# Hand-over rewrite of the stages behind the attention, and another order of the prologue, in a two-block transformer kernel

## The chip, the cores and the metric

The kernel runs on one core of a Trainium2 chip. The metric is the device time of one execution in microseconds (us), as the median of several runs. TensorE is called PE here, VectorE DVE, ScalarE ACT, GpSimd POOL, and SyncE, which issues most of the transfers, SP.

## The reference, cut to what matters

512 tokens of 1024 features pass through two blocks. In the first, 16 learned tokens are put in front, so 528 positions are projected.

```python
def first_block(...):                       # one layer
    u = rmsnorm(h, pre_norm_g)
    proj = u @ w_in                         # 1024 -> cq, ckv, k_pe, z_mla, fq, fk, fv, f_logit, z_fox, gate_a, gate_b
    q = rmsnorm(cq) @ w_uq; kv = rmsnorm(ckv) @ w_ukv        # 16 heads, rotary part of 32
    o_mla = causal_attention(q, k, v)
    cum = cumsum(log_sigmoid(f_logit + fox_forget_b))         # forget gate, enters the second attention
    o_fox = causal_attention(fq, fk, fv, cum)
    mixed = (sigmoid(gate_a) * ((o_mla * silu(z_mla)) @ w_br_mla)
             + sigmoid(gate_b) * ((o_fox * silu(z_fox)) @ w_br_fox)) @ w_out
    return (h + rmsnorm(mixed, post_norm_g))[:, 16:]

def second_block(x, ...):                   # two layers
    # layer 0: xn @ w_in_even -> gated 3-tap convolution (a) and multiscale pooling (b); @ w_out_even; + h
    # then the feed-forward: silu(conv3(hn @ w_gate) + b) * (hn @ w_up), @ w_down; + h   (width 2816)
    # layer 1: gelu(xn @ w_in_odd) -> u, v; gate = tril(w_spatial) @ rms_norm(v) + b_spatial; (u * gate) @ w_out_odd; + h
    # then a feed-forward again
    return rms_norm(h, final_norm)
```

Everything is float32. A product is made exact enough by splitting both operands into a rounded part (HI) and a rest (LO), and adding three products: HI·HI, HI·LO and LO·HI.

## The kernel before, in words

Activations lie transposed: features on the 128 partitions, tokens along the free dimension, as 8 tiles `[128, 512]` (`KT = 8`). A weight **unit** is a panel of 128 output columns by 1024 inputs. `w_load` (SP, L254) brings a unit into one of two raw buffers once the unit two before it has been split, `w_hi` (ACT, L291) rounds it to HI, `w_lo` (DVE, or POOL during the attention, L302) makes LO, and `product` (PE, L331) runs 8 k-tiles by 3 passes, 24 matmuls of 512 columns. Each engine has one program in order; all order between engines is in semaphores, written out by hand. `loop` runs the first and the last body straight and the rest in a hardware loop. The stages in order are:

- **Prologue** (`load_prologue`, `act_prologue`, `pool_prologue`, `dve_prologue`, `pe_prologue`). ACT issues the constants, the meta tokens and the 13 small tables (gains, convolution taps: `dma_small`, L367 to L381), SP issues x and the weights. PE waits for all small tables (L608), transposes them, then the meta tokens (L615), then x (L623, 32 transposes); DVE scales the rows of x (`normalise`, L507), ACT and DVE make HI and LO of the normalised x (`u`). Four units follow: two for cq, one for the forget gate with the rotary key, one for ckv. The forget gate is finished only in `dve_first` and `act_first` of step 0.
- **Steps** 0 to 16 (`steps`): in each, PE interleaves the scores and values of one pair of heads with the projections of the next. Step 0 has no attention and fills q, k, v of pair 0; its DVE program starts with the rotary key's LO (`dve_kpe_lo`, L584), its POOL program makes LO of the rotated queries (L1270) before it splits the first unit of step 1. Step 16 has the last pair and the two gate products of the first mix tile.
- **Mix** (`pe_mix`, `act_mix`, `dve_mix`): 16 gated attention tiles are split (L1423, L1457), then 4 units per output tile.
- **Out** (`pe_out`, `act_out`, `dve_out`): 8 units; x is read again (`x2_in`, behind `mixed`) and transposed (L1654); the squares of the result are added up by POOL (`pool_squares`, L1595), summed over partitions on PE (L1660), turned into 1/rms per token, put on a diagonal and broadcast by PE into bank 7 (L1663). Then DVE runs, for each of 8 tiles, scale (L1714), add (L1716), and LO (`h_low`, L1707).
- **Even** (`pe_even`, `act_even`, `dve_even`): 4 units for the pooling branch, 3, then the pool unit, then 9 for the convolution branch. The broadcast 1/rms comes from a matmul of ones with `acc` (`pe_stats`), a square root and a DVE reciprocal of 512 columns (L1622).
- **Residual products** (`pe_residual` and its companions), **feed-forward** (`*_ffn`), **odd** (`*_odd`: v, spatial weights, u, then the gate: DVE L2147, DVE L2154 multiply by u, ACT L2106 HI, DVE L2161 LO; 2 buffers `odt`), and **final** (`pe_final`, `act_final`, `dve_final`, `load_final`: 32 transposes L2187, ACT scales by 1/rms L2202, DVE multiplies by the gain L2212, SP writes 4 tiles of 512 KB, L2175).

The lines of `out` that the text comes back to:

```python
for n in range(KT):                                   # dve_out
    ...
    dve.tensor_tensor(res_t[:, n % 2, :], m2[:, n, :], bank(7), ALU.mult).then_inc(sem("res"), 1)
    dve.wait_ge(sem("res"), n + 1)
    dve.scalar_tensor_tensor(out=h[:, n, :], in0=res_t[:, n % 2, :], scalar=vcol("post_g", n),
                             in1=h[:, n, :], op0=ALU.mult, op1=ALU.add).then_inc(sem("h_tile"), 1)
    if n:
        h_low(n - 1)
```

## Time and profile before

| | |
|---|---|
| median of 3 runs | 1854.63 us (1853.55 to 1855.92) |
| profiled execution, its own time | 1852.69 us |
| its span, first to last instruction | 1851.0 us |
| PE busy | 1781.2 us, 96% of the span |
| DVE, ACT, POOL busy | 926.5, 766.2, 353.4 us |
| mean granted TensorE clock | 0.987 of full speed |
| DMA | 150.65 MB, 81 GB/s over the span |

The profile is one execution as the hardware profiler saw it. A row of the timeline gives the start, the duration, engine, line, operation, count, and in square brackets how long the engine had been idle before it and who ended that. PE is busy nearly always, so what matters are the stretches in which it is idle, or in which its granted clock is at half: those are read by stage.

### The profile page before, as it was taken

The page shows a single profiled execution, that of the slowest core. Times are in us where ns is not written, and L with a number is a line of the kernel's source. Part 1 is how long each engine was busy: PE and PEld are TensorE (multiplying, and loading weights), DVE is VectorE, ACT ScalarE, POOL GpSimd, SP SyncE. Part 2 cuts the span into 40 slices and gives each one's busy share as a digit, 9 for nine tenths or more (in the row PEclk, how much of TensorE's full clock was granted, in tenths as well). Part 3 has the DMA queues.
Part 4 walks back from the last instruction along what each step waited for, and adds up shares of the span by engine and source line. Part 5 has one row for each costly group of instructions (what it writes and reads, how often), then busy time and mean ns, then how long its engine had stood idle before and what let it go on. Part 6 is the DMA issues. An engine that isn't in the chain of part 4 may idle for free.

```text
span 1851.0 us, 25382 instructions
## 1 busy us (share of the span) xinstructions
PE 1781.2 (96%) x8785; PEld 1475.3 (80%) x8785; DVE 926.5 (50%) x1465; ACT 766.2 (41%) x1332; POOL 353.4 (19%) x383
## 2 busy tenths in 40 slices
PE   7899999999999999979999999999999999999998
PEld 6677778898987888757778888888787878888886
DVE  4656565555555334386555555433336455555322
ACT  4656565554544223333343333322263443333222
POOL 4534435333321000220021111101000211111000
PEclk9999999999999999989999999999999999999998
DMA  4111112121212333413333333333331333333332
GB/s 128 51 42 38 52 42 58 47 59 46 57 46 69 102 91 86 142 46 97 91 91 91 96 96 91 99 95 93 110 93 57 91 98 95 91 101 91 94 95 96
DMA packets 282071, 150.65 MB, mean 81 GB/s; under 512 B 11735, under 2 KB 277970, under 8 KB 282002
## 3 DMA queue, kind: packets, MB, share of 16 engines
q1 hardware_dynamic: 280912, 149.14, 27.9%
q8 instruction: 42, 0.69, 0.2%
q10 hardware_dynamic: 546, 0.40, 0.1%
q0 software_dynamic: 544, 0.20, 0.1%
q14 instruction: 27, 0.22, 0.0%
HBM read 147.54 MB, written 2.16 MB: 81 GB/s over the span
## 4 chain that ended last, share of the span: by engine, by line
PE 85%; DVE 8%; ACT 3%; issue 2%; DMA 1%; POOL 1%; ACTq 0%; POOLq 0%; DVEq 0%; SPq 0%
PE ps L331 65%; PE ps L889 5%; PE ps L770 3%; PE ps L2029 2%; PE ps L747 2%; PE ps L729 2%; PE ps L736 1%; ACT w_split L291 1%; DVE w_split L302 1%; PE ps L776 1%; DVE arena_r L1170 1%; PE ps L783 1%; DVE tmp L1622 1%; DVE u L1707 0%; DVE arena_r L1140 0%
## 5 line engine op out<-in xcount | busy, mean ns | idle before, releaser
L331 PE MATMUL ps<-u,w_split 128*128 128x512 f32 x3888 | 925.2, 396 | 17.2 <-DVE u L1707 7.9
L331 PEld LDWEIGHTS ps<-u,w_split 128*128 128x128 f32 x3888 | 726.2, 189 | 185.3 <-issue 11.3
L302 DVE TENSOR_TENSOR w_split<-w_raw,w_split 128x1024 fp32r<-128x1024 f32 (+1 forms) x221 | 266.8, 1208 | 475.8 <-ACT w_split L291 475.8
L291 ACT CAST w_split<-w_raw 128x1024 fp32r<-128x1024 f32 (+4 forms) x321 | 288.5, 913 | 420.6 <-PE ps L331 353.6
L331 PE MATMUL ps<-arena_r,w_split 128*128 128x512 f32 x1824 | 420.9, 392 | 7.2 <-DVE arena_r L2161 3.0
L331 PEld LDWEIGHTS ps<-arena_r,w_split 128*128 128x128 f32 x1824 | 344.6, 189 | 81.6 <-DVE arena_r L2161 4.8
L302 POOL TENSOR_TENSOR w_split<-w_raw,w_split 128x1024 fp32r<-128x1024 f32 (+3 forms) x100 | 138.1, 1401 | 47.0 <-ACT w_split L291 46.8
L1951 POOL TENSOR_TENSOR tmp<-tmp 128x512 f32<-128x512 f32 x44 | 56.9, 1294 | 424.8 <-ACT tmp L1936 424.8
L955 ACT ACTIVATE tmp<-ps,stats 128x144 f32<-128x144 f32 (+3 forms) x128 | 69.3, 541 | 145.8 <-DVE stats L1127 145.3
L1595 POOL TENSOR_TENSOR tmp<-tmp 128x512 f32<-128x512 f32 x42 | 63.3, 1506 | 281.4 <-ACT tmp L1558 246.5
L889 PE MATMUL ps<-u,w_split 128*128 128x264 f32 x768 | 104.4, 288 | 0.5 <-POOL w_split L302 0.5
L1140 DVE TENSOR_TENSOR arena_r<-ps,arena_r 128x128 fp32r<-128x128 f32 (+3 forms) x128 | 62.8, 491 | 73.2 <-ACT arena_r L971 72.3
L889 PEld LDWEIGHTS ps<-u,w_split 128*128 128x128 f32 x768 | 97.0, 189 | 1.5 <-POOL w_split L302 0.9
L1127 DVE TENSOR_REDUCE stats<-ps 128x1 f32<-128x144 f32 (+3 forms) x128 | 64.3, 502 | 51.3 <-PE ps L731 50.5
L1592 POOL COPY tmp<-tmp 128x512 f32<-128x512 f32 x6 | 4.9, 823 | 439.1 <-ACT tmp L1558 253.3
L1308 POOL TENSOR_TENSOR tmp<-tmp,ones 128x16 f32<-128x16 f32 x128 | 28.2, 220 | 279.7 <-DVE tmp L1135 278.7
L971 ACT CAST arena_r<-ps 128x128 fp32r<-128x128 f32 (+3 forms) x128 | 54.4, 425 | 56.8 <-PE ps L747 55.4
L770 PE MATMUL ps<-arena_r 128*128 128x512 f32 (+3 forms) x384 | 71.9, 329 | 2.4 <-DVE arena_r L1140 2.4
L1936 ACT ACTIVATE tmp<-tmp,vec 128x512 f32<-128x512 f32 x44 | 31.8, 723 | 97.7 <-DVE tmp L1972 97.7
L1972 DVE SCALAR_TENSOR_TENSOR tmp<-tmp,vec 128x512 f32<-128x512 f32 x88 | 65.9, 749 | 5.5 <-DVE tmp L1972 0.3
L770 PEld LDWEIGHTS ps<-arena_r 128*128 128x128 f32 x384 | 58.8, 189 | 8.9 <-DVE arena_r L1140 4.3
L1942 ACT CAST arena_r<-tmp 128x512 f32 (+1 forms) x44 | 27.3, 620 | 87.2 <-DVE tmp L1982 87.2
(233 smaller groups left out, 1541.4 us busy)
## 6 DMA issues: line engine op xcount, KB each, us to landing
w_raw<-in_w_in_dram SPq DMA_DIRECT2D x118, 256.0 KB, 3.1
w_raw<-in_w_ffn_gate_dram SPq DMA_DIRECT2D x88, 256.0 KB, 3.1
w_raw<-in_w_ffn_up_dram SPq DMA_DIRECT2D x88, 256.0 KB, 3.2
w_raw<-in_w_ffn_down_dram SPq DMA_DIRECT2D x64, 256.0 KB, 3.1
w_raw<-in_w_in_even_dram SPq DMA_DIRECT2D x32, 256.0 KB, 3.0
w_raw<-in_w_in_odd_dram SPq DMA_DIRECT2D x32, 256.0 KB, 3.1
w_raw<-in_w_ffn_down_dram SPq DMA_DIRECT2D x32, 192.0 KB, 2.7
w_raw<-in_w_br_mla_dram SPq DMA_DIRECT2D x16, 256.0 KB, 3.1
```

The costliest lines, as they stand in the source:

```text
L291: ins = act.copy(dst, src)
L302: ins = dve.tensor_tensor(lo, r, hi, ALU.subtract)
L331: last = pe.matmul(out_ap, w_tile(c, ws, k - n0), moving(k, ms), start=start and n == 0, stop=stop and n == len(total) - 1, skip_group_che ...
L770: pe.matmul(bank(B_O, j * P, 512), v_t[:, par, vs, j, v_cols(hh)], p_t[:, hh, pp * NQ + j, j * P:512], start=hh == 0 and j == 0 and n == 0 ...
L889: ins = pe.matmul(bank(b, 0, HALF), w_tile(c + j, ws, k), u[:, k, ms, half * HALF:(half + 1) * HALF], start=k == 0 and n == 0, stop=k == K ...
L955: act.activation(probs(b), scored(b), ACT.Exp, bias=neg[:, b:b + 1], accum_out=rs[:, b:b + 1]) \
L971: act.copy(hi, src).then_inc(sem("p_hi"), 1)
L1127: dve.tensor_reduce(neg[:, b:b + 1], scored(b), AX.XY if b % NQ == NQ - 1 else AX.X, ALU.max, negate=True).then_inc(sem("neg"), 1)
L1140: dve.tensor_tensor(lo, src, hi, ALU.subtract).then_inc(sem("p_split"), 1)
L1595: ins = pool.tensor_tensor(acc[:, 0, :], acc[:, 0, :], sq[:, n % 2, :], ALU.add)
L1951: pool.tensor_tensor(cnv[:, j, :], cnv[:, j, :], rbc[:, 0, :], ALU.mult) \
L1972: dve.scalar_tensor_tensor(out=cnv[:, j, :], in0=gpad[:, j, tap:tap + SEQ], scalar=ffn_vec(layer, tap, f), in1=cnv[:, j, :], op0=ALU.mult, ...
```

## The change

All edits keep what is computed. The diff has some 1300 lines; what follows is its core.

1. **Prologue.** The small tables (now 14, with the final norm's gain) move from ACT's queue to SP's, behind x, the constants and the first unit. The unit with the forget gate and the rotary key comes first, in banks 0 and 1; cq follows in banks 2 and 3. The forget gate's chain, the rotary key's HI and LO and the write of the forget rows are finished in the prologue. POOL starts its first split only when x is normalised.
2. **Step 0.** PE runs q before k and v; `dve_kpe_lo` and the forget work leave it; the LO of the rotated queries goes from POOL to DVE.
3. **Mix.** Four of the 16 attention tiles, whose place is free, are split during step 16; PE no longer waits for the last gated tile before the branch product.
4. **Out.** x is read again earlier for tile 0; squares are taken from PSUM; the sums over tokens are taken in two parts, around the last k-tile; 1/rms is broadcast to two banks, and POOL scales three of the eight tiles.
5. **Even.** Token sums, reciprocal of 4 columns, diagonal, broadcast; six convolution units before the pool unit; DVE and ACT programs interleaved in another order.
6. **Odd.** The spatial weights and biases are loaded in the first body of the down product; the gate's multiplication by u goes from DVE to POOL, with four buffers.
7. **Final.** DVE applies the final gain to each tile as it is finished, PE transposes most tiles inside the last product, ACT and DVE scale one half each, SP writes 8 halves.

```diff
@@ dma_x / load_prologue @@
+            for t in range(NQ):
+                sp.dma_start(nat[:, t, :], a["x"][0, t * P:(t + 1) * P, :]).then_inc(sem(f"x_in{t}"), 16)
+                if t == 0:
+                    sp.dma_start(cst[:], consts).then_inc(sem("cst_in"), 16)
...
             dma_x(sp)
-            for t in range(2):
-                w_load(sp, PRO + t, panel(w_in, W_CQ + t * P))
-            sp.wait_ge(sem("vec_tr"), 1)
-            dma_rope(sp)
-            w_load(sp, PRO + 2, [
+            w_load(sp, PRO, [
...
+            dma_vectors(sp)
+            w_load(sp, PRO + 1, panel(w_in, W_CQ))
+            sp.wait_ge(sem("vec_tr"), 1)
+            dma_rope(sp)
+            w_load(sp, PRO + 2, panel(w_in, W_CQ + P))
             w_load(sp, PRO + 3, panel(w_in, W_CKV))
@@ pool_prologue @@
+            pool.wait_ge(sem("x_sc"), 5)
             w_lo(pool, PRO)
...
             for c in range(PRO + 1, PRO + 6):
                 w_lo(pool, c)
+                if c == PRO + 4:
+                    pool_forget(pool)
@@ pe_prologue @@
+            w_ready(pe, PRO)
+            for k in range(KT):
+                pe.wait_ge(sem("u_lo"), max(k, 1) + 2)
+                ins = halves(PRO, (0, 1), (k,), 96)
+            ins.then_inc(sem("w_used"), 1)
...
@@ products_mla, step 0 @@
-                        lambda: (q_rope(), k_and_meta(), q_nope()), v, lambda: z(7, zf, range(KT))]
+                        lambda: (q_rope(), q_nope()), lambda: (k_and_meta(), v()), lambda: z(7, zf, range(KT))]
@@ act_step / dve_step, step 16 @@
+                    elif b in (2, 3):
+                        o_split_hi(act, EARLY_O[2 * b - 4:2 * b - 2])
...
+                if gemm == "gates" and b in (3, 4):
+                    o_split_lo(dve, EARLY_O[2 * b - 6:2 * b - 4])
@@ dve_first @@
-            dve_kpe_lo(dve)
...
+            dve_rope_lo(dve, 0, 0)
             dve_v(dve, 0, "mla", 0)
-            dve_forget_cum(dve)
-            dve_forget_lo(dve)
@@ pe_mix @@
-            pe.wait_ge(sem("gated"), STEPS)
@@ load_out @@
-                if n % 2 == 1:
-                    t = n // 2
-                    if t == 0:
+                for t in {0: (0,), 2: (1, 2), 4: (3,)}.get(n, ()):
+                    if t == 1:
                         sp.wait_ge(sem("mixed"), KT)
@@ pe_out @@
+                    product(pe, bank(n % 4), OUT + n, u_real, range(KT - 1), stop=False)
+                    pe_token_sums(pe, "out", 6, False)
+                    product(pe, bank(n % 4), OUT + n, u_real, (KT - 1,), start=False).then_inc(sem("w_used"), 1)
...
+            pe_token_sums(pe, "out", 6, True)
+            pe.wait_ge(sem("diagonal"), 1)
+            pe.wait_ge(sem("h_x"), KT)
+            for b in (7, 5):
+                pe.matmul(bank(b), ones[:], sq[:, 0, :], start=True, stop=True).then_inc(sem("out_rbc"), 1)
@@ act_out @@
+                act.activation(sq[:, n % 2, :], bank(n % 4), ACT.Square).then_inc(sem("squared"), 1)
...
+            w_hi(act, OUT + KT + 1)
+            act.wait_ge(sem("out_rbc"), 2)
+            act.copy(rbc[:, 0, :], bank(5)).then_inc(sem("out_rsb"), 1)
@@ dve_out @@
+            dve_token_diagonal(dve, "out")
+            w_lo(dve, OUT + KT + 1)
...
+            scale(0)
+            add(0)
+            scale(2)
+            low(0)
+            add(1)
+            add(2)
+            low(1)
...
+        def pool_out(pool):
+            pool.wait_ge(sem("m2"), KT)
+            pool.wait_ge(sem("out_rsb"), 1)
+            for n in POOL_SCALED:                     # 1, 3, 5
+                pool.tensor_tensor(m2[:, n, :], m2[:, n, :], rbc[:, 0, :], ALU.mult).then_inc(sem("res_pool"), 1)
@@ pe_even @@
-            pe_stats(pe, "e")
+            for t in range(NQ):
+                ins = pe.matmul(bank(6, t, t + 1), acc[:, 0, t * P:(t + 1) * P], ones[:, 0:1], start=True, stop=True)
...
+            product(pe, bank(2), EZ + 2, u_real, range(4), stop=False)
+            pe.wait_ge(sem("diagonal"), 2)
+            pe.matmul(bank(7), ones[:], sq[:, 0, :], start=True, stop=True).then_inc(sem("e_bc"), 1)
@@ dve_even, its new order (3 pooling groups, then convolution group 0 ...) @@
+            for g in range(3):
+                pool_mean(g, pool_sums(g))
+                lo()
+                pooled_lo(g)
+            conv_first(0)
+            src = pool_sums(3)
+            conv_second(0)
+            lo()
...
+            for g in (2, 3):
+                conv_first(g)
+                lo()
+                conv_second(g)
+                lo()
+                conv_taps(g)
+                conv_third(g)
+                lo()
+                y_lo(g)
@@ load_odd -> load_spatial, called in the first body of the down product @@
+        def load_spatial(sp):
+            sp.wait_ge(sem("h_tile"), KT)
...
+            sp.wait_ge(sem("ffn_a_lo"), FT)
@@ dve_odd -> pool_gate @@
-                dve.tensor_tensor(y, y, m2[:, hd, :], ALU.mult).then_inc(sem("gate_y"), 1)
...
+                y = y_bufs[hd % 4]
+                pool.tensor_tensor(y, y, m2[:, hd, :], ALU.mult).then_inc(sem("gate_y"), 1)
@@ final @@
+                    sp.wait_ge(sem(f"fin{half}"), t + 1)
+                    sp.dma_start(out[t * P:(t + 1) * P, cols], y_out[t][:, cols]).then_inc(sem("stored"), 16)
...
+        def pe_final_early(pe, m):
+            if m == 0:
+                pe.wait_ge(sem("fin_sc"), 6)
...
+                act.activation(y_out[t][:, 0:SEQ], bank(FIN_BANK[t, 0]), ACT.Copy, scale=rtok[:, t:t + 1]) \
...
+                dve.tensor_scalar(y_out[t][:, SEQ:D], bank(FIN_BANK[t, 1]), rtok[:, t:t + 1], None, ALU.mult) \
```

`pe_token_sums` makes four matmuls with a moving operand of one column, either from `acc` (seven tiles) or from the last squares; `dve_token_diagonal` is the reciprocal of four columns and the diagonal of 512.

## Rows read from the trace of the kernel before

**Rows 1.** The page's busy time, share and instructions of each engine.

```profile
PE 1781.2 (96%) x8785; PEld 1475.3 (80%) x8785; DVE 926.5 (50%) x1465; ACT 766.2 (41%) x1332; POOL 353.4 (19%) x383
```

**Rows 2.** Stretches: length, PE, PEld, DVE, ACT, POOL busy, TensorE clock, DMA.

```profile
541.00:568.90 27.90, 24.41 (x138) 19.46 (x137) 16.11 (x40) 13.16 (x31) 8.91 (x11) 0.99 0.16 40
...
784.00:814.20 30.20, 18.69 (x60) 12.28 (x59) 23.19 (x30) 13.80 (x22) 13.50 (x9) 0.77 0.06 18
814.20:900.00 85.80, 82.22 (x351) 65.40 (x351) 56.76 (x75) 25.23 (x32) 0.00 (x0) 1.00 0.32 94
...
1312.20:1409.80 97.60, 94.79 (x417) 77.00 (x415) 40.51 (x44) 48.19 (x69) 1.33 (x1) 0.98 0.34 103
1409.80:1431.10 21.30, 18.17 (x110) 15.11 (x110) 18.03 (x26) 5.59 (x9) 0.00 (x0) 0.86 0.09 25
...
1835.00:1851.00 16.00, 7.90 (x40) 7.27 (x40) 5.84 (x10) 7.01 (x11) 1.26 (x1) 0.71 0.32 131
```

**Rows 3.** Timeline of the prologue: start, us, engine, line, [idle before <- releaser].

```profile
6.53 0.39 ACTq L381 DMA_DIRECT2D tmp<-in_b_conv_ffn_dram  x1
...
11.46 0.36 PE L608 MATMUL ps<-cst,tmp 75*128 75x75 f32 x1 [11.46 <-DMA tmp<-in_b_conv_ffn_dram]
...
13.01 6.54 PE L623 MATMUL ps<-cst,big 128*128 128x128 f32 x32
```

**Rows 4.** Timeline of step 0.

```profile
58.40 5.54 DVE L584 TENSOR_TENSOR arena_r<-big,arena_r 32x528 fp32r<-32x528 f32 x4
...
68.19 4.42 POOL L302 TENSOR_TENSOR w_split<-w_raw,w_split 128x256 fp32r<-128x256 f32 x6 [1.73 <-ACT w_split L291]
...
72.66 1.69 PE L808 MATMUL ps<-arena_r,w_split 128*128 128x264 f32 x6 [4.83 <-POOL w_split L302]
```

**Rows 5.** Groups of instructions, 541 to 582 us: busy, mean ns | idle before.

```profile
L331 PE MATMUL ps<-arena_r,w_split 128*128 128x512 f32 x48 | 12.5, 424 | 2.3 <-DVE arena_r L1457 2.3
...
L1457 DVE TENSOR_TENSOR arena_r<-big,arena_r 128x512 fp32r<-128x512 f32 x16 | 9.7, 689 | 0.8 <-ACT arena_r L1423 0.8
L1423 ACT CAST arena_r<-big 128x512 fp32r<-128x512 f32 x16 | 8.4, 615 | 2.5 <-DVE big L1189 2.5
```

**Rows 6.** Timeline of the out stage and of the even stage's first product.

```profile
741.77 0.66 PE L1654 MATMUL ps<-cst,tmp 128*128 128x128 f32 x4 [1.28 <-DMA tmp<-in_x_dram]
...
795.17 5.06 PE L331 MATMUL ps<-u,w_split 128*128 128x512 f32 x10 [3.70 <-DVE u L1707]
```

**Rows 7.** Groups of instructions, 784 to 815 us.

```profile
L1707 DVE SCALAR_TENSOR_TENSOR u<-big,vec,u 128x512 fp32r<-128x512 f32 x8 | 9.0, 1129 | 0.1
```

**Rows 8.** Timeline from 798 us: DVE and POOL side by side.

```profile
798.01 1.28 POOL L1595 TENSOR_TENSOR tmp<-tmp 128x512 f32<-128x512 f32 x1 [0.46 <-ACT tmp L1687]
...
799.76 0.74 DVE L1707 SCALAR_TENSOR_TENSOR u<-big,vec,u 128x512 fp32r<-128x512 f32 x1
...
801.19 1.83 POOL L1595 TENSOR_TENSOR tmp<-tmp 128x512 f32<-128x512 f32 x1 [1.90 <-ACT tmp L1687]
...
801.80 1.77 DVE L1707 SCALAR_TENSOR_TENSOR u<-big,vec,u 128x512 fp32r<-128x512 f32 x1
```

**Rows 9.** Groups of instructions, 814 to 908 us.

```profile
L331 PE MATMUL ps<-u,w_split 128*128 128x512 f32 x338 | 78.9, 394 | 2.9 <-DVE w_split L302 2.9
...
L331 PE MATMUL ps<-arena_r,w_split 128*128 128x512 f32 x26 | 6.4, 395 | 2.0 <-DVE arena_r L1883 2.0
```

**Rows 10.** Timeline: the spatial weights' transposes in the odd stage.

```profile
1322.67 1.94 PE L2040 MATMUL ps<-cst,big 128*128 128x128 f32 x8 [2.62 <-DMA big<-in_w_spatial_dram]
```

**Rows 11.** Groups of instructions, 1409 to 1432 us: the gate.

```profile
L2154 DVE TENSOR_TENSOR tmp<-tmp,big 128x512 f32<-128x512 f32 x8 | 5.5, 691 | 0.3
L2161 DVE TENSOR_TENSOR arena_r<-tmp,arena_r 128x512 fp32r<-128x512 f32 x8 | 5.5, 686 | 0.1
```

**Rows 12.** Groups of instructions, 1834 to 1851 us.

```profile
L2187 PE MATMUL ps<-cst,big 128*128 128x128 f32 x32 | 6.5, 387 | 0.8 <-DVE big L1579 0.8
```

**Rows 13.** Timeline of SP's queue at the end.

```profile
1841.97 6.30 SPq L2175 DMA_DIRECT2D out_dram<-tmp  x4
```

More of the change, by code:

```diff
@@ L1059, in act_v, with o_split_hi, o_split_lo @@
             ins.then_inc(sem("v_hi"), 1)
+        EARLY_O = (0, 1, 4, 5)
+        O_ORDER = EARLY_O + tuple(t for t in range(16) if t not in EARLY_O)
+        def o_split_hi(act, tiles):
+            act.wait_ge(sem("gated"), max(tiles) + 1)
+            act.wait_ge(sem("scores"), 8 * (STEPS - 1))
+            for t in tiles:
+                act.copy(o_r[:, t, HI, :], big[:, t, :]).then_inc(sem("o_hi"), 1)
+        def o_split_lo(dve, tiles):
+            for t in tiles:
+                dve.wait_ge(sem("o_hi"), O_ORDER.index(t) + 1)
+                dve.tensor_tensor(o_r[:, t, LO, :], big[:, t, :], o_r[:, t, HI, :], ALU.subtract) \
+                    .then_inc(sem("o_lo"), 1)
         def act_first(act, c, nxt):
@@ L1415, in body @@
                         moving = lambda k, part, j=j: o_r[:, 8 * (j - 2) + k, part, :]
-                    ready = (lambda k: pe.wait_ge(sem("o_lo"), 8 * (j - 2) + k + 1)) if first else None
-                    product(pe, bank(j), c, moving, ready=ready).then_inc(sem("w_used"), 1)
+                    ready = (lambda k: pe.wait_ge(sem("o_lo"), O_ORDER.index(8 * (j - 2) + k) + 1)) if first else None
+                    ks = [t for t in O_ORDER if t < KT] if first and j == 2 else range(KT)
+                    product(pe, bank(j), c, moving, ks, ready=ready).then_inc(sem("w_used"), 1)
             loop(pe, KT, body)
@@ L1421, in act_mix @@
             act.wait_ge(sem("gated"), STEPS)
-            for t in range(16):
-                act.copy(o_r[:, t, HI, :], big[:, t, :]).then_inc(sem("o_hi"), 1)
+            o_split_hi(act, O_ORDER[len(EARLY_O):])
             def body(n, first, last):
@@ L1484, in tiles_before, with acc_before @@
             return KT * NORMS.index(tag)
+        def acc_before(tag):
+            return tiles_before(tag) - (1 if tag != "out" else 0)
         def hs_before(tag):
@@ L1534, in body @@
                             k0 += ks
+                if first and after_first:
+                    after_first(sp)
             loop(sp, KT // 2, body)
@@ L1587, in pool_squares @@
         def pool_squares(pool, tag):
-            for n in range(KT):
+            for n in range(KT - 1 if tag in ("out", "down1") else KT):
                 pool.wait_ge(sem("squared"), tiles_before(tag) + n + 1)
@@ L1607, in pe_stats, with pe_token_sums, dve_token_diagonal @@
             ins.then_inc(sem("summed"), 1)
+        def pe_token_sums(pe, tag, b, last):
+            if not last:
+                pe.wait_ge(sem("acc_done"), acc_before(tag) + KT - 1)
+            else:
+                pe.wait_ge(sem("squared"), tiles_before(tag) + KT)
+            src = sq[:, 1, :] if last else acc[:, 0, :]
+            for t in range(NQ):
+                ins = pe.matmul(bank(b, t, t + 1), src[:, t * P:(t + 1) * P], ones[:, 0:1],
+                                start=not last and t == 0, stop=last, skip_group_check=True)
+            if last:
+                ins.then_inc(sem("summed"), 1)
+        def dve_token_diagonal(dve, name):
+            dve.reciprocal(rtok, sstok).then_inc(sem("rbc"), 1)
+            dve.wait_ge(sem("rbc"), norms_done(name))
+            dve.tensor_tensor(sq[:, 0, :].rearrange("p (t n) -> p t n", t=NQ),
+                              ident.rearrange("p (a n) -> p a n", a=1).to_broadcast([P, NQ, P]),
+                              rtok.rearrange("p (t a) -> p t a", a=1).to_broadcast([P, NQ, P]), ALU.mult) \
+                .then_inc(sem("diagonal"), 1)
         def act_stats(act, tag, bc=True, tok=False):
```

559 lines of the change are left out of this document (311 added, 248 removed).

## Prediction

> **What bounds the kernel now.** I read the page first. PE is busy for 1781.2 of 1851.0 us [rows 1]: nothing else comes near, so a change can give back only what PE loses, and that is at most 70 us of idle time plus what the half clock costs. The change removes no product. The next view is therefore the timeline of PE alone, for its idle gaps, and then the stretches around them with their clock. The reader should see that the long middle parts are dense and that the losses sit at the seams. In the out stage's end PE idles 11.5 of 30.2 us and has a mean clock of 0.77, which is 30.2 x 0.23 / 0.5 = 13.9 us at the lower of its two levels, 1.2 instead of 2.4 GHz. The even stage loses 3.6 us, the odd stage 2.8, the gate at its end 3.1 (with 6.0 us at half clock), the final stage 8.1 of 16.0, and step 16 3.5 [rows 2]. Outside those are 4.8 us before step 1 [rows 4], 2.3 before the mix [rows 5] and 1.3 in the out stage [rows 6]. The chain of the end runs through them all, since each stage needs the whole result of the one before: a microsecond saved at a seam is a microsecond of the total.
>
> **Prologue and step 0.** Now the last small table is issued at 6.5 to 6.9 us on ACT's queue and has landed at 11.46, which PE waits for; the 32 transposes of x follow at 13.0 at 0.20 us each and end at 19.5 [rows 3]. In the new order 14 tables stand on SP's queue behind 2 MB of x, the constants and two scattered transfers. At 0.39 us for an issue [rows 3] the 14 take 5.5 us after some 4.5 us for the others, so the last is issued near 10 and lands, with the 1 to 4.5 us that bracket landing here (less would put it before its data; 4.5 is what the last one needed amid the x traffic), at 11 to 14.5. I take 12.2, since x is through by then: a loss of 0.7. POOL's first split then no longer meets DVE's scaling of x, and x waits nowhere. The sums of cq now come behind each other at the unit's end, and I count 1.2 us of idle time in place of 1.45 in three small ones. PE enters step 0's q about 1.2 us later than before. In step 0 the rotary LO of 5.54 us (it shares time with POOL) is gone from the front of DVE's program, and with it the queue behind it: k and q LO, the copy of v, ACT's HI of the next unit, POOL's 4.42 us [rows 4]. From the start of q I count, with the durations that the same instructions have in the timeline, 3.1 us for q, 4.6 to k, then ACT's k, q, rotary, v and the unit's HI (1.5 + 1.2 + 1.2 + 0.9 + 1.3), ending at 10.8, and POOL's 3.0 (alone) to 4.4 (beside DVE) [rows 4]: 14.5, against 17.4 before. So step 1's first product comes 2.9 - 1.2 = 1.7 us earlier, and its wait is some 2 instead of 4.8. The six matmuls there take 1.69 us [rows 4], at half clock; half of the 1.9 us that this costs may go, say 0.8. **Term: -2.5**, between +1 (tables at 14.5, clock as now) and -5.
>
> **Step 16 and mix.** The gap of 2.3 us goes, since four tiles cover 4 x 0.70 us of product while the 12 others are split, and so does the slow start: 48 matmuls took 12.5 us [rows 5], against 48 x 78.9 / 338 = 11.2 at the even stage's rate [rows 9]. A shortfall of 0.5 comes back where the next unit's split is queued behind these. That is -3.1. But four HI copies of 0.62 us and four LO of 0.69 [rows 5] stand in step 16 in front of ACT's and DVE's work for the softmax of blocks 2 to 4. There the chain from maximum to exponential, scaling and the split of the transposed block is as long as PE's work for a block: DVE is busy only 16.1 of 27.9 us, yet PE idles 3.5 [rows 2]. Behind the inserted work wait the maximum of the next block, and for it PE's transposes and scores. Bounds 0 and 5.2 (all of both); I take 2.6. **Term: -0.5.**
>
> **Out stage.** The wait for x of 1.28 us goes [rows 6]. From the last product's end (784.0) to the first even product it takes 11.2 us now [rows 6]. The new chain, by the rows' 0.62 for ACT and 0.69 for DVE: sums of seven tiles 0.9, square 0.6, sums of the last 1.0, root 0.2, reciprocal 0.2, diagonal 0.7, broadcast 0.5; then DVE's split of the next unit, which waits for ACT's HI and ends 1.2 later; scale, add, scale, LO 2.9. That is 8.2. For the remaining 17 DVE operations the neighbour counts: beside a POOL operation on SBUF data a LO takes 1.77 us instead of 0.74, and ends 0.55 after POOL's end; POOL itself takes 1.83 instead of 1.28 [rows 8], so that 8 LOs have a mean of 1.13 [rows 7]. 16 such DVE operations at 0.55 and 10 of POOL at 1.15 make 20.3 us from POOL's first scaling (about 5.6 after the product's end): the last LO ends at 26, against 28.2 now, and PE is less far behind. I take 3.0 for this. **Term: -4.3**, between -2.5 and -6.5.
>
> **Even.** Four gaps of 2.9 us wait for a split unit, each behind a long DVE passage; one of 2.0 waits for the last tile [rows 9]. Walking the new order with 0.69 per operation and 1.2 per split, every split ends before PE needs it, the closest (the unit behind the pool unit) by 0.4 us; the last tile's LO is 3.4 us behind the last unit, covered by seven k-tiles of 5.1. The broadcast adds 0.5 of PE. The first of the four gaps, 1.0, stays, because the split behind it starts no earlier after the product before. 4.9 - 1.0, less 0.5 and plus 0.4 for shorter sums: **Term: -3.8**, between -2 and -4.9.
>
> **Odd.** The spatial weights are there in time: the wait of 2.62 goes, and with it 3.9 us at half clock [rows 2, 10], worth 2.0. **Term: -4.6**, between -2.6 and -4.8.
>
> **Gate.** DVE needs 0.75 + 0.69 + 0.69 = 2.1 per head now, the last two of them its multiply and LO [rows 11], and PE waits for the last LO. With POOL at 1.28 and LO at 0.69 the cycle is 1.3 if they overlap, 2.0 if each has to wait for the other in full, and 1.7 if they overlap only where rows 8 show it (1.15 + 0.55). Eight heads then end 7 x 0.4 = 2.8 us earlier, less 1.1 for a longer first pass, plus a part of the 6.0 us at half clock. **Term: -2.0**, between +1 and -4.7.
>
> The Trainium skill, in "SBUF — State Buffer", section "SBUF: two separate sides", says that a GpSimd operation and a DVE operation with two SBUF inputs exclude each other, and that whoever starts first keeps the port for the whole instruction. Rows 8 agree on the exclusion. By the rule taken with whole instructions the cycle would be 1.28 + 0.69 = 1.97, the gate would give nothing and the total would be 1837.5; by the rows' own overlap it is 1835.5.
>
> **Final.** 22 of the 32 transposes and half of the sums move into the last product; the group shows 0.20 per transpose, mostly at half clock [rows 12], so at full clock 0.14: 3.1 + 0.9 = 4.0 us more before the last product ends. Behind it: add 0.7, square 0.6, sums 1.0, root and reciprocal 0.4, first scaling 0.7, first output at +3.6. The four outputs of now are issued over 6.3 us and end 2.7 after the last issue [rows 13]; The DMA share of 0.32 over 16.0 us [rows 2] is 5.1 us of all engines for the same bytes; with some 0.9 before the first byte and 0.9 behind the last, from the timeline, the end is at +10.5. 14.5 in place of 16.1. **Term: -1.6**, between +1 and -4.
>
> **Sum.** -2.5 - 0.5 - 4.3 - 3.8 - 4.6 - 2.0 - 1.6 = -19.3. The profiled execution's own time is 1852.7 (span 1851.0 and 1.7 around it), the median 1854.6, 1.9 above; 1852.7 - 19.3 + 1.9 = 1835.3, rounded to 1835.5.
>
> **Rivals.**
> - *The new waits eat half.* Step 16 loses 5.2 instead of 2.6, the tables land at 14.5, the gate's cycle is 2.0, the final stage gives nothing: +2.6 + 2.3 + 2.0 + 1.6 gives 1844. For it: each is a bound above. Against it: they are independent.
> - *More comes back.* Wherever a gap shrinks below 2 us the clock stays up, the gate's cycle is 1.3: the lower bounds of three terms, 1828. For it: all long stretches at half clock follow a gap; against it, several short gaps in a row also bring it down at the gate.
> - *The tables land one after the other.* If each of the 14 on SP's queue had to land before the next moves, each would cost the 2.7 us that the last output needed from issue to end [rows 13]: 9.5 + 38 = 47, PE starts 36 us later, and the total is 1871. It decides from a landing at about 31 us. Against it: the last of 13 tables was there 4.6 us after its issue ended, in time for two such steps and not for 13 [rows 3].
> - *No change,* because a wait not seen in the trace takes all: 1854.
>
> **Chances.** Forecast 0.70, half eaten 0.13, more 0.10, tables 0.04, no change 0.03. The range of 1827 to 1845 holds the first three and leaves out their tails and the last two. A measurement of this kernel can tell 0.2%, 3.7 us, from no change: faster 0.93, within it 0.03, slower 0.04.
>
> **What would show it.** PE's start on the tables at 12 to 13 us; step 1's first product near 71; no gap before the mix, but longer blocks in step 16; no gap at the x transposes; first even product 8 us behind the last out product; no split waits in the even stage; no gap at the spatial transposes, and full clock there; POOL multiplies of 1.3 to 1.8 in the gate; first output 3.6 us behind the last product. I am wrong if the tables land after 15 us, if step 16 grows by more than 4, or if DVE and POOL block each other in the gate for longer than 2 us a head.

## The result and the profile after

The changed kernel takes 1836.11 us (median of 4 runs, 1835.23 to 1838.53), the kernel before 1855.28 on the same chip (4 runs, 1853.55 to 1856.79): ratio 0.990, 95% interval 0.988 to 0.991. The forecast was 1835.5. The profiled execution took 1835.31 (span 1833.6), which is 17.4 below that of before.

The first part of the page of the changed kernel answers to [rows 1]: a little less PE, because less of it runs at half clock, and no other engine nearer to the bound.

```profile
PE 1774.6 (97%) x8811; PEld 1470.5 (80%) x8811; DVE 922.1 (50%) x1461; ACT 765.1 (42%) x1333; POOL 359.3 (20%) x390
```

What follows is PE's timeline of the changed kernel, the first rows of the stretches in which the prediction saw losses.

```profile
15.81 0.37 PE L605 MATMUL ps<-cst,tmp 83*128 83x83 f32 x1 [15.81 <-DMA tmp<-in_b_conv_ffn_dram]
...
73.04 1.00 PE L806 MATMUL ps<-arena_r,w_split 128*128 128x264 f32 x6 [1.68 <-POOL w_split L302]
...
566.88 0.96 PE L774 MATMUL ps<-arena_r 48*128 48x512 f32 x3
567.77 1.43 PE L331 MATMUL ps<-arena_r,w_split 128*128 128x512 f32 x5
...
784.70 3.46 PE L1718 MATMUL ps<-tmp,ones 128*128 128x512 f32 x4 [1.20 <-DVE tmp L1656]
790.89 2.05 PE L331 MATMUL ps<-u,w_split 128*128 128x512 f32 x6 [2.73 <-DVE u L1776]
795.18 4.64 PE L331 MATMUL ps<-u,w_split 128*128 128x512 f32 x12 [2.25 <-DVE u L1776]
...
813.46 3.04 PE L331 MATMUL ps<-u,w_split 128*128 128x512 f32 x12 [1.03 <-DVE w_split L302]
...
952.03 8.36 PE L331 MATMUL ps<-u,w_split 128*128 128x512 f32 x35 [1.02 <-DVE w_split L302]
...
1412.09 0.97 PE L331 MATMUL ps<-arena_r,w_split 128*128 128x512 f32 x3 [0.72 <-DVE arena_r L2336]
...
1823.09 0.55 PE L2356 MATMUL ps<-cst,big 128*128 128x128 f32 x3 [0.79 <-DVE big L1605]
```

The reader should see what is gone (the waits of 2.32 and 1.28 [rows 5 and 6], all waits for a split between 814 and 952, the wait of 2.62 [rows 10]), what has shrunk (4.83 [rows 4] to 1.68) and what has come: the tables land at 15.81, and at the out stage's end PE still waits 2.73, 2.25, and then 0.28, 1.58, 1.58 and 1.03.

With the same row in both timelines as a milestone, the difference after minus before can be cut into the prediction's terms. The milestones are step 16's first score (540.74, 539.90), the out stage's first product (734.80, 733.40), the third unit of the even stage, which is the first behind the two that run tile by tile as their LO comes (816.27, 813.46), the first unit behind even_out that waits (959.44, 952.03), the gate's first product (1408.38, 1396.57), the unit behind odd_out that waits (1483.08, 1467.12), and the spans.

| term | predicted | bounds | read |
|---|---|---|---|
| prologue, step 0, on to step 16 | -2.5 | -5 to +1 | -0.84 |
| step 16, mix | -0.5 | | -0.56 |
| out | -4.3 | -6.5 to -2.5 | **-1.41** |
| even | -3.8 | -4.9 to -2 | -4.60 |
| odd | -4.6 | -4.8 to -2.6 | -4.40 |
| gate | -2.0 | -4.7 to +1 | -4.15 |
| final | -1.6 | -4 to +1 | -1.44 |
| sum | -19.3 | | -17.4 |

Two terms fell short, by 4.6 us together, and even and gate gave 2.9 more. The experiments ask why.

### The profile page after: what moved, and what is told of

Read it like the earlier page. It is cut to its first block, busy times and chain, and to the rows that moved or that the text cites. A ratio compares the mean times of both kernels' runs of the same rounds, so it can differ in the third digit from the quotient of the medians.

```text
span 1833.6 us, 25452 instructions
## 1 busy us (share of the span) xinstructions
PE 1774.6 (97%) x8811; PEld 1470.5 (80%) x8811; DVE 922.1 (50%) x1461; ACT 765.1 (42%) x1333; POOL 359.3 (20%) x390
## 4 chain that ended last, share of the span: by engine, by line
PE 89%; DVE 5%; ACT 3%; issue 1%; POOL 1%; SPq 1%; DMA 0%; DVEq 0%; ACTq 0%; POOLq 0%
PE ps L331 68%; PE ps L888 5%; PE ps L768 3%; PE ps L2196 2%; PE ps L745 2%; PE ps L727 2%; PE ps L734 1%; PE ps L774 1%; PE ps L781 1%; PE ps L629 1%; ACT w_split L291 1%; DVE w_split L302 1%; DVE arena_r L1185 1%; DVE big L1771 0%; DVE arena_r L1155 0%
## 5 line engine op out<-in xcount | busy, mean ns | idle before, releaser
L2116 POOL TENSOR_TENSOR tmp<-tmp 128x512 f32<-128x512 f32 x44 | 56.9, 1294 | 424.8 <-ACT tmp L2101 424.8
L1625 POOL TENSOR_TENSOR tmp<-tmp 128x512 f32<-128x512 f32 x40 | 56.8, 1421 | 269.5 <-ACT tmp L1584 234.5
```

The costliest lines, as they stand in the source:

```text
L1625: ins = pool.tensor_tensor(acc[:, 0, :], acc[:, 0, :], sq[:, n % 2, :], ALU.add)
L2116: pool.tensor_tensor(cnv[:, j, :], cnv[:, j, :], rbc[:, 0, :], ALU.mult) \
```

## The experiments

The experiments ran on three chips, on which the kernel before has medians of 1855.99, 1856.03 and 1854.63. The intervals of the ratios of experiments 1 to 6 and 9 overlap that of the changed kernel, so their medians alone do not separate them from it: each is judged by its stretch of the profile, which is one execution. All ratios are against the kernel before.

**1 and 2. Where the small tables are issued.** The prediction let the last table land at 12.2. In the changed kernel SP's queue shows one issue of 3.69 us, right behind the unit with the forget gate and the rotary key, whose two transfers have rows of 64 and 128 bytes:

```profile
4.48 1.63 SPq L254 DMA_DIRECT2D w_raw<-in_w_in_dram  x2
6.15 3.69 SPq L379 DMA_DIRECT2D tmp<-in_pre_norm_g_dram  x1
9.89 0.25 SPq L379 DMA_DIRECT2D tmp<-in_mla_q_norm_g_dram  x1
```

One kernel issues the tables on ACT's queue again:

```diff
@@ load_prologue @@
-            dma_vectors(sp)
@@ act_prologue @@
             act.dma_start(nat[0:META, 4, :], a["meta_tokens"]).then_inc(sem("meta_in"), 16)
+            dma_vectors(act)
```

> The changed kernel with one thing undone: the 14 small tables are issued on ACT's queue behind the meta tokens, as the kernel before did, and not on SP's behind x and the scattered forget unit. Theory (the prologue term failed because SP's queue stalls: the first table's issue was held for 3.69 us and the last table landed at 15.81 instead of 12.2): the tables land at 11 to 12, the transposes of x start 13 to 13.5 instead of 17.4, the first product comes near 20.3 instead of 24.1, and the total falls by 3 to 4 us, to about 1832.5. Rival (the tables are not what counts, step 1's wait for POOL's split takes the gain): the first product comes earlier but step 1's wait grows from 1.68 by as much, total as now, 1836.

The other leaves them on SP's, but ahead of that unit:

```diff
@@ load_prologue @@
             dma_x(sp)
+            dma_vectors(sp)
             w_load(sp, PRO, [
...
-            dma_vectors(sp)
```

> The changed kernel with the 14 tables still on SP's queue, but issued right behind x and the constants, ahead of the scattered unit with the forget gate and the rotary key (two transfers with short rows). Theory A (it is the scattered unit, whose two issues took 1.63 us and whose many small pieces fill the queue, that held the first table's issue for 3.69 us): the stall is gone from the tables, they land near 11, start -3 us or more, unless the unit itself then comes late; about 1833. Theory B (the queue is full from x, 2 MB): the first table is held all the same, to about 8 us, the last lands at 13 to 14, and -1 to -2 us are left: about 1834.5.

On ACT's queue: 1833.05 us (1829.8 to 1833.56), ratio 0.988 (0.986 to 0.990); the tables land at 11.21, the first product starts at 20.68, step 1's at 68.04 with a wait of 1.70. Ahead of the unit: 1831.67 us (1830.7 to 1834.02), ratio 0.988 (0.986 to 0.990); SP's queue and PE in this kernel:

```profile
3.33 0.41 SPq L379 DMA_DIRECT2D tmp<-in_pre_norm_g_dram  x1
...
11.94 0.37 PE L605 MATMUL ps<-cst,tmp 83*128 83x83 f32 x1 [11.94 <-DMA tmp<-in_b_conv_ffn_dram]
...
68.72 1.00 PE L806 MATMUL ps<-arena_r,w_split 128*128 128x264 f32 x6 [1.68 <-POOL w_split L302]
```

The issue behind x takes 0.41 us and no other table's takes longer than 0.42: the 2 MB of x alone do not stop the queue. Nor does the scattered unit alone. Its two issues and the next unit's two are one row, first of this kernel and then of experiment 1, where they stand right behind x:

```profile
8.39 2.20 SPq L254 DMA_DIRECT2D w_raw<-in_w_in_dram  x4
```

```profile
3.49 6.80 SPq L254 DMA_DIRECT2D w_raw<-in_w_in_dram  x4
```

The same four take 4.6 us more when x is still on its way. In the changed kernel the packets of x (4096 bytes) run until 9.85 us, the first of the scattered unit moves at 8.64, and the held issue ends at 9.84; here the unit is issued when x is nearly through (9.57). So what holds the queue is the scattered unit standing behind a large transfer. In the profiles of five experiments below that keep the changed kernel's order, the first table's issue was held for 2.87 to 4.08 us and the tables landed at 14.96 to 16.39. With the stall away they land at 11.94. That is close to the 12.2 that was assumed, but in part by luck, since here the last is issued at 7.99 and not near 10. Step 1 starts 4.3 us earlier. The rival (step 1's wait grows instead) falls: it stays at 1.7.

**3. POOL's three scalings in the out stage, back to DVE.**

```diff
-        POOL_SCALED = (1, 3, 5)
+        POOL_SCALED = ()
@@ dve_out @@
-            scale(0)
...
+            for n in range(KT):
+                scale(n)
+                add(n)
+                if n:
+                    low(n - 1)
+            low(KT - 1)
```

> The changed kernel with the three POOL scalings in the out stage given back to DVE: all 8 tiles scaled, added and made LO on DVE, in the order of the kernel before. Theory (the out term failed because POOL's scalings and DVE's two-input operations exclude each other: one scaling of three took 4.64 us, a DVE add 1.7 instead of 0.69): DVE's 24 operations at 0.7 each take 17 us beside POOL's squares, and the point two units behind the first even product moves by no more than 1 us either way; if DVE is quicker without POOL, by -1 us. Rival (POOL's three scalings save 3 of DVE's 24 operations for nothing): the point comes 2.1 us later, total 1838.

1832.92 us (1830.69 to 1835.63), ratio 0.988 (0.986 to 0.990). From the broadcast (784.70 and 786.28) to the third even unit (813.46 and 812.66) it takes 26.38 us instead of 28.76; before it was 26.88. So POOL's help, with the order of DVE's operations that went with it, cost 2.4 us, more than the 1 us that the theory allowed, and the rival, which made it worth 2.1, has the wrong sign. The span of this profile (1833.9) does not show it: it was 1.6 us behind when the broadcast began, and lost 1.1 in the second feed-forward (see the last section). The groups of the end of the out stage (784 to 814), changed kernel first (columns as in [rows 5]):

```profile
L1771 DVE SCALAR_TENSOR_TENSOR big<-big,vec 128x512 f32<-128x512 f32 x8 | 10.8, 1381 | 0.0
L1776 DVE SCALAR_TENSOR_TENSOR u<-big,vec,u 128x512 fp32r<-128x512 f32 x8 | 8.2, 1025 | 1.9 <-ACT u L1740 1.7
L1806 POOL TENSOR_TENSOR big<-big,tmp 128x512 f32<-128x512 f32 x3 | 4.6, 1571 | 12.0 <-ACT tmp L1737 12.0
```

and with all scalings on DVE:

```profile
L1776 DVE SCALAR_TENSOR_TENSOR u<-big,vec,u 128x512 fp32r<-128x512 f32 x8 | 9.0, 1128 | 0.2
L1771 DVE SCALAR_TENSOR_TENSOR big<-big,vec 128x512 f32<-128x512 f32 x8 | 6.9, 868 | 0.3
L1764 DVE TENSOR_TENSOR big<-big,ps 128x512 f32<-128x512 f32 x8 | 5.4, 678 | 0.3 <-PE ps L1718 0.3
```

A scaling on DVE reads one of its two operands from PSUM, takes 0.68 us and is not held. Three of them save 2.0 us of DVE when they go to POOL. For that the eight adds (L1771) take 1.38 instead of 0.87 us each, 4.1 us more; the LOs (L1776) get 0.8 back, and DVE is idle for 1.7 us more, mostly waiting for ACT's HI.

**4. What POOL's other work costs there.** POOL also adds up the squares of h during that stretch. On top of the kernel of experiment 3 these additions are cut down from 512 columns to 8, which leaves the sum of squares incomplete:

```diff
@@ pool_squares @@
-                    ins = pool.tensor_tensor(acc[:, 0, :], acc[:, 0, :], sq[:, n % 2, :], ALU.add)
+                    w = 8 if tag == "e" else SEQ
+                    ins = pool.tensor_tensor(acc[:, 0, 0:w], acc[:, 0, 0:w], sq[:, n % 2, 0:w], ALU.add)
```

> The changed kernel with the scalings of the out stage on DVE, and with POOL's additions of the squares of h in that stage cut from 512 columns to 8, so that the sum of squares, and with it the norm of the even stage, is incomplete: POOL's share of the SBUF work beside DVE's 16 two-input operations is taken away. Theory (the lengthened DVE operations, LO 1.13 us in the mean and add 0.87 where they take 0.75 alone, are held by POOL's additions): all 16 take 0.75, and the time from the broadcast to the second unit of the even stage falls from 26.4 by about 4 us, less what PE's products then bound. Rival (they are long from DVE's own pipeline or from ACT's reads of the same tile): they stay at 1.1 and 0.87, and the stage stays as long.

1829.85 us (2 runs), ratio 0.987 (0.985 to 0.989). The same groups now:

```profile
L1772 DVE SCALAR_TENSOR_TENSOR big<-big,vec 128x512 f32<-128x512 f32 x8 | 6.0, 751 | 0.3
L1777 DVE SCALAR_TENSOR_TENSOR u<-big,vec,u 128x512 fp32r<-128x512 f32 x8 | 6.0, 747 | 0.2
L1765 DVE TENSOR_TENSOR big<-big,ps 128x512 f32<-128x512 f32 x8 | 5.4, 680 | 0.7 <-PE ps L1719 0.7
```

All 16 operations take 0.75, and the stretch (784.61 to 807.42) is 22.81 us, 3.6 less, as expected. This shows the exclusion by taking it away, and the rival (DVE's own pipeline, or ACT's reads) falls: 28.8 us with eleven POOL operations beside DVE, 26.4 with eight, 22.8 with next to none.

**5. The early split in step 16, undone.** All 16 attention tiles are split at the start of the mix.

```diff
@@ act_step / dve_step @@
-                    elif b in (2, 3):
-                        o_split_hi(act, EARLY_O[2 * b - 4:2 * b - 2])
...
-                if gemm == "gates" and b in (3, 4):
-                    o_split_lo(dve, EARLY_O[2 * b - 6:2 * b - 4])
```

> The changed kernel without the early split: no attention tile is split in step 16, all 16 at the start of the mix. Theory (what the hand-over gains, step 16 pays): step 16 is 2.1 us shorter, the wait of 2.3 us ahead of the mix product and 0.3 to 0.5 of slow start come back, total within 0.7 us of the changed kernel, 1836.5. Rival (the longer step 16 has another cause, such as the new start of the step or the clock): step 16 stays as long and the wait comes back, total 1838.7.

1836.35 us (1835.47 to 1840.18), ratio 0.991 (0.988 to 0.993). PE's timeline of this kernel, in which step 16 begins at 539.97:

```profile
564.85 0.96 PE L774 MATMUL ps<-arena_r 48*128 48x512 f32 x3
568.17 1.17 PE L331 MATMUL ps<-arena_r,w_split 128*128 128x512 f32 x4 [2.37 <-DVE arena_r L1072]
```

From the step's start to its last value product it is 24.88 us, to the hundredth that of the kernel before, against 26.98 with the early split; to the first mix product 28.20 against 27.87; to the out stage's broadcast 244.84 against 244.80. So the early split moves a wait of 2.4 us out of the seam and into the softmax chain, and is worth nothing.

**6. The gate's multiplication back on DVE.**

```diff
@@ dve_odd @@
                                          op0=ALU.mult, op1=ALU.add).then_inc(sem("gate"), 1)
+                dve.wait_ge(sem("gate"), hd + 1)
+                dve.wait_ge(sem("ou"), hd + 1)
+                dve.tensor_tensor(y, y, m2[:, hd, :], ALU.mult).then_inc(sem("gate_y"), 1)
                 if hd >= 2:
@@ pool @@
-            pool_gate(pool)
```

> The changed kernel with the gate's multiplication by u given back to DVE (between DVE's scaling and its LO, the four buffers kept) and nothing left to POOL there. Theory (the gate gained because POOL and DVE overlap as far as rows 8 show, 1.70 us a head against DVE's 2.1 to 2.2): the distance between two heads grows to 2.1 to 2.2, seven distances cost 2.8 to 3.5, less about 1.1 for a shorter first pass: total +2 us, about 1838. Rival (what the milestone at the gate gained came from the early spatial weights and the clock, POOL against DVE is even): +0.5 us at most.

1838.04 us (1834.86 to 1839.68), ratio 0.991 (0.989 to 0.993); the medians differ by 1.9 us from the changed kernel, but the runs overlap. DVE's timeline there, one head, ahead of the same in the changed kernel:

```profile
1405.39 0.68 DVE L2339 TENSOR_TENSOR arena_r<-tmp,arena_r 128x512 fp32r<-128x512 f32 x1
1405.99 0.75 DVE L2317 SCALAR_TENSOR_TENSOR tmp<-ps,vec,tmp 128x512 f32<-128x512 f32 x1
1406.77 0.69 DVE L2324 TENSOR_TENSOR tmp<-tmp,big 128x512 f32<-128x512 f32 x1
1407.38 0.68 DVE L2339 TENSOR_TENSOR arena_r<-tmp,arena_r 128x512 fp32r<-128x512 f32 x1
```

```profile
1404.15 1.11 DVE L2336 TENSOR_TENSOR arena_r<-tmp,arena_r 128x512 fp32r<-128x512 f32 x1
1405.18 0.74 DVE L2317 SCALAR_TENSOR_TENSOR tmp<-ps,vec,tmp 128x512 f32<-128x512 f32 x1
1405.84 1.11 DVE L2336 TENSOR_TENSOR arena_r<-tmp,arena_r 128x512 fp32r<-128x512 f32 x1
```

The distance of two heads is 1.99 us on DVE alone (the theory had 2.1 to 2.2) and 1.69 with POOL. The gate starts 0.43 us earlier in this profile, so the times are counted from DVE's first operation of the gate (1399.24, and 1399.67 in the changed kernel). On DVE alone the first LO begins after 4.2 instead of 2.8 us (1403.40, 1402.46), but the last three, with nothing else left for DVE, take 1.89 us together, where those paced by POOL take 3.62: the last ends after 16.00 instead of 14.88 us (1415.24, 1414.55), 1.1 later. In the kernel before it ends after 17.34 us, so 1.3 us of the gate's gain come from the new order with four buffers and not from POOL. From the gate's first product to the unit behind odd_out that waits it takes 74.22 us (1396.14 to 1470.36) instead of 70.55, and most of these 3.7 us is the clock: behind waits of 1.01, 1.03 and 0.65 us PE's granted clock is 0.80 and 0.88 from 1407.2 to 1416 and to 1430, where the changed kernel shows 1.00.

**7. POOL's multiplication done twice per head.**

```diff
@@ pool_gate @@
+                pool.tensor_tensor(sq[:, 1, :], y, m2[:, hd, :], ALU.mult).then_inc(sem("gate_x"), 1)
+                pool.wait_ge(sem("gate_x"), hd + 1)
                 pool.tensor_tensor(y, y, m2[:, hd, :], ALU.mult).then_inc(sem("gate_y"), 1)
```

> The changed kernel with POOL's multiplication in the gate done twice per head: first into an unused buffer, then as before. It doubles the suspected cost. Theory (a POOL and a DVE operation with two SBUF inputs exclude each other, but a DVE operation ends 0.55 us behind POOL's end, so that a head costs 1.15 + 0.55): each further POOL operation adds 1.15 to 1.3 us a head, the distance is 2.85 to 3.1, the total +8 to +10 us, about 1845. Rival 1 (no exclusion at all, DVE is the bound at about 1.9): the distance is POOL's two operations alone, 2.56, total +6. Rival 2 (the whole instruction locks): 2 x 1.28 + 0.69 = 3.25, and each DVE instruction behind it starts only when POOL's has ended, total +11.

1848.3 us (1845.31 to 1850.42), ratio 0.996 (0.995 to 0.997), 12.2 above the changed kernel. POOL and DVE of one head:

```profile
1407.69 1.28 POOL L2332 TENSOR_TENSOR tmp<-tmp,big 128x512 f32<-128x512 f32 x1
1408.42 1.10 DVE L2338 TENSOR_TENSOR arena_r<-tmp,arena_r 128x512 fp32r<-128x512 f32 x1 [1.16 <-ACT arena_r L2273]
1409.05 1.62 POOL L2334 TENSOR_TENSOR tmp<-tmp,big 128x512 f32<-128x512 f32 x1
1410.64 1.25 POOL L2332 TENSOR_TENSOR tmp<-tmp,big 128x512 f32<-128x512 f32 x1
1411.35 1.09 DVE L2338 TENSOR_TENSOR arena_r<-tmp,arena_r 128x512 fp32r<-128x512 f32 x1 [1.17 <-ACT arena_r L2273]
```

The distance is 2.93 us: within the 2.85 to 3.1 of the theory, beyond the 2.56 of POOL alone and short of 3.25. How the two take turns can be read here: DVE's LO is on record at 1408.42, in the middle of POOL's operation, and ends at 1409.52, 0.55 behind POOL's end at 1408.97; POOL's next is on record at 1409.05 and ends 1.15 behind DVE's end. Each is held by the other, but some 0.13 us of either row (1.28 - 1.15, 0.69 - 0.55) lie outside what is locked. The total is nearer to rival 2's +11 than to the theory's +8 to +10, since more comes in than the seven distances add (8.7 us): the first LO is later too, so that the last ends after 25.26 us of the gate instead of 14.88, and behind it another 2.4 us are lost, where the last four of PE's groups of three products between two waits run at half clock (1.65 instead of 0.97 us each). The distance, not the total, decides between the rivals.

**8. The early spatial weights alone, in the kernel before.**

```diff
@@ load_odd, before @@
-                if m == 1:
-                    sp.wait_ge(sem("h_tile"), hs_before("down0") + KT)
-                    sp.dma_start(bbc[:, 0, :], a["b_spatial_2"].rearrange("a h t -> a (h t)").to_broadcast([P, D])) \
-                        .then_inc(sem("b_in"), 16)
-                    sp.dma_start(m2[:, 0:2, :].rearrange("p a (b s) -> p (a b) s", s=P),
-                                 a["w_spatial_2"][0].rearrange("h t s -> t h s")).then_inc(sem("ws_in"), 16)
@@ load_residual, with load_spatial as after_first for down0 @@
+                if first and after_first:
+                    after_first(sp)
```

> The kernel before with one part of the change alone: the spatial weights and their bias are loaded in the first body of the first down product instead of behind the second unit of the odd stage. Theory (the wait of 2.62 us and the half clock that follows it are all of the odd term): the wait is gone, the clock stays up, -4.6 us, about 1850.5. Rival (the gain of 5.8 us read at the odd stage came from other edits that also touch it, such as the statistics of tokens): -2.6 us or less, half clock as before.

1850.37 us (1848.11 to 1852.87), ratio 0.998 (0.996 to 0.999). PE's timeline, which answers to [rows 10]:

```profile
1319.83 1.07 PE L2044 MATMUL ps<-cst,big 128*128 128x128 f32 x8
1320.66 9.53 PE L2033 MATMUL ps<-w_split,u 128*128 128x512 f32 x40
```

No wait, and eight transposes in 1.07 instead of 1.94 us. The first product of the odd stage starts at 1312.13 (1312.21 before), the gate's at 1403.90 instead of 1408.38, the waiting unit behind odd_out at 1478.21 instead of 1483.08: 4.4 us for this edit up to the gate and 4.8 with it, where the theory had 4.6.

**9 and 10. What the findings give together.** First the tables ahead of the unit and the scalings on DVE (experiments 2 and 3):

> The changed kernel with two edits that alone gained: the tables ahead of the scattered unit on SP's queue (-4.4 us in the median), and all eight scalings of the out stage on DVE (in the profile -2.3 us in that stage). Theory (both are seams of the chain, and what a seam gives adds up): 1836.1 - 4.4 - 2.3 = 1829.4. Rival (the clock takes part of it back at the next gap): 1831.5.

1831.43 us (1830.56 to 1833.11), ratio 0.988 (0.987 to 0.990). Seen by the median it is no better than experiment 2 alone (1831.67). In its profile both gains are there: the stretch from broadcast to third even unit is 25.88 us, and step 1 starts at 70.55, only 2.5 earlier, since the tables landed at 12.72 this time and the clock fell in step 0 (0.83 from 50 to 60, where it was 1.00 in experiment 2). The rival's 1831.5 is the nearer one; of its cause, the clock, the profile shows about 1 us, and the later landing 0.8.

Then PE and DVE treat x before the tables are there:

```diff
@@ dve_prologue @@
             normalise(0, NQ)
-            normalise(1, 0)
+            for t in range(NQ):
+                normalise(t + 1, t)
             dve.wait_ge(sem("vec_tr"), 1)
@@ pe_prologue, the meta tokens' transposes now ahead of this @@
+            for t in range(NQ - 1):
+                x_tiles(t, range(6))
             pe.wait_ge(sem("vec_in"), N_VEC_DMA)
...
             ins.then_inc(sem("vec_tr"), 1)
+            x_tiles(NQ - 1, range(6))
+            pe.wait_ge(sem("meta_t"), 2)
+            for t in range(NQ):
+                x_tiles(t, (6, 7))
```

> The last kernel (tables ahead of the scattered unit, scalings on DVE) with one more edit: PE transposes the meta tokens and x, and DVE normalises all of x, before either of them waits for the small tables; only the two x tiles whose banks the tables use come behind them. Theory (PE and DVE stood idle until the tables landed at about 12, though x was there from 5 to 11 us): ACT's first HI of the normalised x starts near 13.5 instead of 19.1, the first product near 15.5 instead of 21.4, and all behind it moves: -5.5 us, about 1826. Rival (the tables are only one of several late things, and POOL's split of the first unit, which waits for x and for ACT's HI, then sets the start): first product at 18 or later, -3 us, about 1828.5.

1827.51 us (4 runs, 1826.34 to 1828.96) against 1854.63 before: ratio 0.986, interval 0.984 to 0.987. It is the fastest here, 8.6 us below the changed kernel. PE's timeline:

```profile
16.66 3.51 PE L634 MATMUL ps<-u,w_split 128*96 128x264 f32 x27 [1.52 <-POOL w_split L302]
...
67.24 1.00 PE L811 MATMUL ps<-arena_r,w_split 128*128 128x264 f32 x6 [1.69 <-POOL w_split L302]
```

The first product is 4.96 us earlier than in experiment 9's kernel (16.66 against 21.62), near the theory's 15.5, though its releaser is now POOL's split, as the rival said. Step 1 starts only 3.3 us earlier: the clock between 20 and 60 is 0.91 instead of 0.96. The median gains 3.9.

## Why the prediction was right, and which terms were off

- **What bounds the kernel**: right. No product was removed; what was gained was gained at seams, and in experiments 2, 8 and 10 the span falls by 4.1, 4.6 and 4.3 us where the seam gained 4.3, 4.8 and 3.3 (the rest of the last is the feed-forward's 1.1).
- **Prologue and step 0 (-2.5, read -0.84): two steps wrong, with opposite signs.** The first is "the 14 take 5.5 us after some 4.5 us for the others, so the last is issued near 10". The first was issued at 6.15 and held for 3.69 us behind the scattered unit, the last followed at 14.1, and they landed at 15.8: 3.6 us later than assumed, behind the bound of 14.5 and behind the 15 us that the prediction names as a sign that it is wrong. For this term that sign was right. The second is the walk through step 0. From the start of q to step 1's first product it counts 14.5 us, and it took 12.9 (60.14 to 73.04, against 17.4 before), with a wait of 1.68 (some 2 predicted) and six matmuls in 1.00 instead of 1.69 us. Together step 1 came 0.4 us later than before, not 1.7 earlier, and from there to step 16 the kernel gained 1.2 (0.8 predicted). With the stall away step 1's first product is at 68.7, even earlier than "near 71".
- **Step 16 and mix (-0.5, read -0.56): right**, and by its own two parts: step 16 lost 2.10 (2.6 predicted), the seam gained 2.66 (3.1).
- **Out (-4.3, read -1.41): outside its bounds.** The first even product is 9.1 us behind the out stage's last, where the prediction had 8 and the kernel before has some 11. Ahead of POOL's first scaling "broadcast 0.5" was wrong: it took 3.46 us for four matmuls, behind waits, and the scaling began 7.2 us behind the product's end (781.75), not 5.6. Behind it "16 such DVE operations at 0.55 and 10 of POOL at 1.15" made 20.3 and took 21.0: that price held, and the last LO ends 28.2 us behind the product's end instead of 26, as late as the kernel before's. What the sum did not ask is what the same DVE operations would take with fewer POOL operations between them. Experiment 3 shows that moving three scalings to POOL costs 2.4 us. With them on DVE the term is -3.8, near the forecast.
- **Even (-3.8, read -4.6): right in mechanism.** No split wait is left between 813 and 952; the extra 0.8 was not tested.
- **Odd (-4.6, read -4.40): right.** From the odd stage's first product to the gate's, the changed kernel and that of experiment 8 take 91.77 us each, the kernel before 96.17.
- **Gate (-2.0, read -4.15): inside its bounds, but twice the size.** The cycle was predicted as 1.7 and is 1.69. What was mis-sized is the rest. From DVE's first operation to the end of the last LO it takes 14.88 instead of 17.34 us, 2.5 less, where seven distances of 0.4 less 1.1 made 1.7; by experiment 6 the new order gives 1.3 of it and POOL 1.1. The other 1.7 us is PE's clock, which the prediction had as "a part of the 6.0 us at half clock" and took as 0.3: the waits there are 0.21, 0.72 and 0.72 us, where the timeline of before has 1.22, 1.21 and 0.54, and the clock does not fall.
- **Whole instructions or the rows' overlap.** Experiment 7's distance is 2.93 us, where whole instructions make 2 x 1.28 + 0.69 = 3.25 and the rows' overlap 1.28 + 1.15 + 0.55 = 2.98; the gate's is 1.69 and not 1.97. The Trainium skill has in "SBUF — State Buffer", section "SBUF: two separate sides", that POOL and a DVE operation with two SBUF inputs exclude each other, and with that these rows and experiment 4 agree; where it has the port held for the whole instruction, the measurement decides otherwise: by these rows an instruction is on record some 0.13 us longer than it excludes the other.
- **Final (-1.6, read -1.44): right**, with the parts off: the first output is issued 4.4 us behind the product's end (1822.30) instead of 3.6. ACT loads a table for 1.28 us there before it takes the last squares.
- **The total** came within 0.6 us, and part of that is luck: 4.6 us of misses met 2.9 us of extra gains, which with the small terms left the sum 1.9 short, and the prediction added 1.9 us for the distance of the median from the profiled execution, where that of the changed kernel is 0.8. Two rivals show themselves in part. Of "the new waits eat half" the tables landed late and the other three did not happen; of "more comes back" the clock stayed up in the gate, but its cycle was not 1.3.

## What to carry to other kernels

In the out stage three DVE operations given to POOL saved 2.0 us and made their neighbours, which read two operands from SBUF, 4.1 us longer: price such a move by what the remaining DVE operations become, not by what it takes away. A transfer of many short rows behind a large one held the queue for 2.9 to 4.1 us here, so whatever is small and urgent is better issued ahead of it. And work put into another stage to empty a seam must be priced by the chain it lands in: here it cost 2.1 us and saved 2.4.

## What had not been expected of the hardware

- The stretch of the feed-forward's gate and up products, from the unit that waits behind even_out or odd_out to the first down product, takes one of two values: 231.93 to 231.96 us or 233.06 to 233.07, in the same code and at a granted clock of 1.00 (both values occur in the first and in the second feed-forward, over 12 profiled kernels). What decides is open. Through it alone the spans of two profiles can lie up to 2.3 us apart.
- Short spells of half clock in steps 0 to 5 differ between kernels whose code there is the same: from 176 to 184 us the clock was 0.79 in the changed kernel and 0.57 with the scalings on DVE, and the first waiting unit of the mix stood at 579.72 and 581.24 although the tables had landed earlier in the second (15.40 against 15.81). This is why a gain of 2 us is read in its stretch and not in the total.
